# One decoder step on one core: the gate branch ahead of the fourth query tile, the recurrent channel sum ahead of the third key tile

## The reference, cut to what matters

```python
h = rms_norm(x, lp['norm1_g']) * (1.0 + scale1) + shift1
z = h @ lp['w_in']
x_lru, g_lru, q_lat, kv_lat, k_rope = jnp.split(z, IN_SPLITS, axis=-1)
hs, h_last = rg_lru(causal_dwconv(x_lru, ...), ...)          # scan over the tokens
lru_out = hs * jax.nn.gelu(g_lru)                            # the gate branch
q = (rms_norm(q_lat, ...) @ lp['w_uq'])                      # 8 heads, then q norm and rope
kv_lat = rms_norm(kv_lat, ...)                               # keys and values: kv_lat @ w_ukv
attn = attend(q_nope, q_rope, kv_lat, k_rope)                # prompt, and paged cache for the 8 sequences
mixed = jnp.concatenate([rms_norm(lru_out, lp['lru_out_norm_g']), rms_norm(attn, ...)]) @ lp['w_o']
x = x + gate1 * mixed
x = x + gate2 * ((gelu(gt) * val) @ lp['w_down'])            # behind norm2 and w_up with a short conv
```

## Time and profile before

| | us |
|---|---|
| median of 3 runs | 946.93 (945.82 to 947.53) |
| profiled execution, its own time | 949.23 |
| its span, first to last instruction | 947.4 |
| TensorE busy | 919.8 (97%) |
| VectorE busy | 637.4 (67%) |
| ScalarE busy | 513.1 (54%) |
| GpSimd busy | 184.3 (19%) |

### The profile page before, as it was taken

The page is one execution under the profiler, slowest core; times in us unless marked ns, Lnnn a source line. Parts: engine busy times, 40 slices in busy tenths (PEclk is TensorE's granted clock), DMA queues, the critical chain, the costliest instruction groups (busy, mean ns, idle before and its releaser), DMA issues.

```text
span 947.4 us, 20112 instructions
## 1 busy us (share of the span) xinstructions
PE 919.8 (97%) x7805; PEld 858.7 (91%) x7805; DVE 637.4 (67%) x1241; ACT 513.1 (54%) x1147; POOL 184.3 (19%) x163
## 2 busy tenths in 40 slices
PE   5899999999999999999999989999999999999998
PEld 3588876799999999999899979999999999999997
DVE  2893378488888888888863667777777777722321
ACT  2414845689889889898863354444444443311111
POOL 0032323333333324333330301100000001000000
PEclk9999999999999999999998999999999999999999
DMA  9996732300212203202130423333333331653202
GB/s 338 332 281 222 223 134 102 146 2 23 91 59 77 90 24 112 90 24 90 46 91 23 113 60 90 89 89 90 92 96 98 97 97 50 161 153 80 63 1 91
DMA packets 107897, 100.12 MB, mean 106 GB/s; under 512 B 7125, under 2 KB 96597, under 8 KB 105770
## 3 DMA queue, kind: packets, MB, share of 16 engines
q1 hardware_dynamic: 104030, 77.91, 28.1%
q0 software_dynamic: 3456, 20.97, 6.2%
q10 hardware_dynamic: 340, 0.27, 0.1%
HBM read 96.41 MB, written 2.94 MB: 105 GB/s over the span
## 4 chain that ended last, share of the span: by engine, by line
PE 88%; DVE 6%; ACT 2%; DMA 2%; issue 1%; SPq 0%; POOL 0%; DVEq 0%; ACTq 0%; POOLq 0%
PE ps L890 51%; PE ps L1286 20%; PE ps L885 6%; PE ps L1247 2%; PE ps L1183 2%; PE ps L923 2%; DMA RW<-w_ada 2%; PE ps L1062 1%; PE ps L896 1%; PE ps L1282 1%; DVE RB L1996 1%; PE ps L1209 1%; DVE input_low L1929 1%; DVE up_weights_low L2371 0%; DVE small L1970 0%
## 5 line engine op out<-in xcount | busy, mean ns | idle before, releaser
L890 PE MATMUL ps<-normed_high,up_weights_high 128*128 128x260 f32 x704 | 142.5, 284 | 2.5 <-DVE normed_low L2392 2.4
L890 PE MATMUL ps<-normed_high,up_weights_low 128*128 128x260 f32 x704 | 142.5, 284 | 0.0
L890 PE MATMUL ps<-normed_low,up_weights_high 128*128 128x260 f32 x704 | 142.1, 284 | 0.0
L1791 ACT ACTIVATE up_weights_high<-RW 128x1024 fp32r<-128x1024 f32 x44 | 46.6, 1061 | 128.0 <-PE ps L890 128.0
L836 POOL TENSOR_TENSOR latents_low<-RB,latents_high 128x512 fp32r<-128x512 f32 x64 | 82.7, 1292 | 165.7 <-ACT latents_high L1667 165.6
L1286 PE MATMUL ps<-key_weights_high,latents_high 128*128 128x260 f32 x512 | 113.3, 302 | 0.1
L890 PEld LDWEIGHTS ps<-normed_high,up_weights_high 128*128 128x128 f32 x704 | 108.9, 189 | 3.1 <-issue 2.2
L890 PEld LDWEIGHTS ps<-normed_high,up_weights_low 128*128 128x128 f32 x704 | 109.1, 189 | 0.0
L890 PEld LDWEIGHTS ps<-normed_low,up_weights_high 128*128 128x128 f32 x704 | 108.7, 189 | 0.0
L1286 PE MATMUL ps<-key_weights_high,latents_low 128*128 128x260 f32 x512 | 103.1, 283 | 0.0
L1286 PE MATMUL ps<-key_weights_low,latents_high 128*128 128x260 f32 x512 | 103.1, 283 | 0.0
(11 more groups left out here) (350 smaller groups left out, 2069.5 us busy)
## 6 DMA issues: line engine op xcount, KB each, us to landing
RW<-w_ada SPq DMA_DIRECT2D x24, 1024.0 KB, 7.0
RW<-w_up SPq DMA_DIRECT2D x44, 512.0 KB, 5.1
RW<-w_down SPq DMA_DIRECT2D x8, 1408.0 KB, 7.3
RW<-w_in SPq DMA_DIRECT2D x11, 512.0 KB, 6.4
RB<-w_o SPq DMA_DIRECT2D x8, 512.0 KB, 4.2
RB<-x_prompt SPq DMA_DIRECT2D x2, 1024.0 KB, 12.2
o_y_p<-RB SPq DMA_DIRECT2D x4, 448.0 KB
cst<-consts SPq DMA_DIRECT2D x1, 844.5 KB, 12.0
```

What stands on the lines that cost most here:

```text
L890: last = mm(ps[j % 4][rows[0]:rows[1], h, 0:H], lhsT, src[:, h * H:(h + 1) * H], start=start, stop=stop)
L1791: A(wuH[:, KT * g:KT * g + KT, :], wup[:, c, KT * g:KT * g + KT, :], ACT.Copy).then_inc(s_whi, 1)
```

## The change

The order of work on four engines is written differently; no product, sum or copy is added. TensorE issues four groups fewer: `keep_busy(spare, 3)` and four times `keep_busy(spare, 1)` are gone.

- TensorE: `w_in(11)` and the last chunk of w_ada stand ahead of `queries(3)`. The channel sum `J_NLRU` stands ahead of `keys_and_values(2)`, in PSUM buffer 3 instead of 1.
- ScalarE: the GELU stands ahead of the squares of query tile 3; `lru_squares` stand around that tile's root; the root of the channel sum stands ahead of the third key tile.
- VectorE: the fourth query tile and `mod_columns(5)` stand behind the product with the gate; `split_queries(0)` and `lru_normed` stand ahead of the copies into `QBD`.
- GpSimd: `kwL` is made there; the second sequence's gather stands behind the three additions.

The diff, cut:

```diff
+               "q2", "w11", "q3", "kv0", "kv1"])
+PREP_ORDER = [("c5", 3), ("qst", 3), ("nlru", 3), ("kv2", 1), ("qa", 3), ("kv3", 2), ("spread", 0), ("l0", 3), ("l1", 0),
+              ("l2", 3), ("l3", 0), ("l4", 3), ("l5", 0), ("l6", 3)]
...
+            pool.wait_ge(s_kw, 2)
+            for e in range(2):
+                nc.gpsimd.tensor_tensor(kwL[:, e, :, 0:4 * NOPE], wkn[:, :].rearrange("p (g n) -> p g n", g=2),
+                                        kwH[:, e, :, 0:4 * NOPE].bitcast(F32), ALU.subtract).then_inc(s_kw, 1)
...
-            for n in range(2):
-                cached_keys(n, n)
-                cached_latents(n, n)
-
+            cached_keys(0, 0)
+            cached_latents(0, 0)
+            nc.gpsimd.memset(QBD[:, :, :, :], 0.0).then_inc(s_bdz, 1)
             for k in range(1, LT):
...
+            cached_keys(1, 1)
+            cached_latents(1, 1)
...
             queries(2)
-            queries(3)
             w_in(11)
             later_chunk(15)
+            queries(3)
...
+            claim(pe, J_NLRU)
+            pe.wait_ge(s_lrn, LT - 1)
+            both(J_NLRU, ones, lru_sq[:, 0, :], True, True).then_inc(psum_full[J_NLRU % 4], 1)
             keys_and_values(2)
...
-            keep_busy(spare, 3)
             pe.wait_ge(s_kr, 2)
-            for a in range(4):
+            for a in range(5):
                 stored_rows(a)
-                keep_busy(spare, 1)
...
-            prep_squares(J_Q[3], query_sq, HEADS * QK)
-            prep_rstd(4, 2 * HEADS)
...
+            prep_squares(J_Q[3], query_sq, HEADS * QK)
+            act.wait_ge(s_lrud, 2)
+            lru_squares(0)
+            prep_rstd(4, 2 * HEADS)
+            lru_squares(2)
             key_squares(0)
             key_squares(1)
-            act.wait_ge(s_lrud, 2)
-            lru_squares(0)
             prep_rstd(5, HEADS)
-            lru_squares(2)
             prep_rstd(6, HEADS)
+            rstd(J_NLRU, LW).then_inc(s_rs, 1)
             key_squares(2)
...
+            prep_sums(3, query_sq, HEADS)
+            prep_query_tile(2)
+            mod_rows(5)
+            dve.wait_ge(s_g, 1)
+            V.tensor_tensor(GG[:, :, :], TA[:, :, :], GG[:, :, :], MUL).then_inc(s_lrud, 1)
+            prep_sums(4, query_sq, HEADS)
+            prep_query_tile(3)
             dve.wait_ge(s_kr, 2)
             dve.wait_ge(s_qtok, 4)
             V.tensor_copy(headk[NOPE:QK, :], krT[NOPE:QK, 0:NP]).then_inc(s_krk, 1)
...
-            mod_rows(5)
             mod_columns(5)
-            dve.wait_ge(s_g, 1)
-            V.tensor_tensor(GG[:, :, :], TA[:, :, :], GG[:, :, :], MUL).then_inc(s_lrud, 1)
             full(dve, J_QST)
...
             key_sums(2)
+            dve.wait_ge(psum_free[J_QA % 4], free_value(J_QA))
+            split_queries(0)
+            dve.wait_ge(s_rs, 5)
+            lru_normed()
             full(dve, J_SPREAD)
```

More of the change, by code:

```diff
@@ L1641, in _ @@
                 stored_rows(a)
-            rstd(J_NLRU, LW).then_inc(s_rs, 1)
             stored_rows(4)
@@ L2114, in _ @@
                 V.tensor_copy(kwH[:, e, :, 0:4 * NOPE], wk2).then_inc(s_kw, 1)
-            dve.wait_ge(s_kw, 2)
-            for e in range(2):
-                V.tensor_tensor(kwL[:, e, :, 0:4 * NOPE], wk2, kwH[:, e, :, 0:4 * NOPE].bitcast(F32), SUB).then_inc(s_kw, 1)
             mod_columns(4)
-            for a in range(2, 4):
-                prep_sums(1 + a, query_sq, HEADS)
-                prep_query_tile(a)
+            prep_sums(3, query_sq, HEADS)
[5 more added lines that the diff above has]
+            prep_query_tile(3)
             dve.wait_ge(s_kr, 2)
@@ L2139, in prep_keys, with lru_normed, split_queries @@
                 dve.sem_inc(psum_free[j % 4], 1)
-            mod_rows(5)
+            def lru_normed():
+                for k in range(LT):
+                    V.scalar_tensor_tensor(hT[:, k, :], GG[:, k, :], pr("lru_out_norm_g", k), rs[:, :], MUL, MUL).then_inc(s_mix, 1)
+            def split_queries(u):
+                e = u % 2
+                q = QA[:, u, :].rearrange("p (g h) -> p g h", g=2)
+                V.tensor_copy(kwH[:, e, :, 4 * NOPE:KWW], q).then_inc(s_kwq, 1)
+                dve.wait_ge(s_kwq, 2 * u + 1)
+                V.tensor_tensor(kwL[:, e, :, 4 * NOPE:KWW], q, kwH[:, e, :, 4 * NOPE:KWW].bitcast(F32), SUB).then_inc(s_kwq, 1)
             mod_columns(5)
-            dve.wait_ge(s_g, 1)
-            V.tensor_tensor(GG[:, :, :], TA[:, :, :], GG[:, :, :], MUL).then_inc(s_lrud, 1)
             full(dve, J_QST)
@@ L2171, in _ @@
             prep_keys(3)
-            def lru_normed():
-                for k in range(LT):
-                    V.scalar_tensor_tensor(hT[:, k, :], GG[:, k, :], pr("lru_out_norm_g", k), rs[:, :], MUL, MUL).then_inc(s_mix, 1)
             def by_key(x):
@@ L2216, in finish @@
                 V.tensor_copy(OLR[:, u - 1, :], bank("pv")[:, 0:KV]).then_inc(is_free("pv"), 1)
-            def split_queries(u):
-                e = u % 2
-                q = QA[:, u, :].rearrange("p (g h) -> p g h", g=2)
-                V.tensor_copy(kwH[:, e, :, 4 * NOPE:KWW], q).then_inc(s_kwq, 1)
-                dve.wait_ge(s_kwq, 2 * u + 1)
-                V.tensor_tensor(kwL[:, e, :, 4 * NOPE:KWW], q, kwH[:, e, :, 4 * NOPE:KWW].bitcast(F32), SUB).then_inc(s_kwq, 1)
             def row_max(u, name, blocks):
@@ L2314, in unit @@
                             split_queries(u + 1)
-            split_queries(0)
             for e in range(2):
@@ L2320, in _ @@
             st.seq(V.memset(new_scores[:, :, :], NEG))
-            dve.wait_ge(s_rs, 5)
-            lru_normed()
             for u in range(NS):
```

5 lines of the change are left out of this document (removed).

## The result

The changed kernel took 956.84 us in the median of 4 runs (953.97 to 958.91), the kernel before beside it 947.23 (945.82 to 949.31, 4 runs): ratio 1.0092, 95% interval 1.0071 to 1.0113. It is slower, by more than the 951.5 forecast and just outside the range (947.2 to 956.0).

What follows compares the result with a forecast made beforehand. TensorE was taken to bound the kernel, so only the start of the decode units (first key product) could move the time. Order +1.5, clock +1.6 and +1.5 gave +4.6 us on the 946.93 median: 951.5, range 947.2 to 956.

Steps and rivals of the forecast that it cites:

- two falls of the clock: TensorE's clock at 0.50 near 165, over channel sum and key tiles, and again near 180, into transposes and first keys.
- the second wait: TensorE ahead of the second stored tile: a wait of 2 us or more, released by VectorE's copies into QBD.
- order at full clock: TensorE up to the first transpose: the new order delays it from 178.45 to 180.0, +1.5 us.
- lock on SBUF: GpSimd additions beside VectorE's rotation of query tile 3, 161.0 to 165.2: taken as 0, at most one addition, 1.4 us.
- clock: TensorE's clock falling after the waits: 1.6 us over channel sum and key tiles, 1.5 over transposes and first keys.
- The wait ahead of `J_QST`: TensorE from 160.7, after the second key tile: waits about 4.4 us, released by VectorE's mod_columns(5).
- `kwL` on GpSimd: Moved to GpSimd, idle until 157.18: costs nothing, and gains nothing by taking some 1.2 us off VectorE ahead of a wait.
- The gathers: First sequence's 2.5 us earlier, nothing waiting; second's issued about 165 to 169, cost between 0 and 4.1 us, taken as 0.
- Full clock: Rival: TensorE's clock does not fall, or falls only where it waits anyway; +1.5 us, 948.4, chance 0.14.
- The tail doesn't matter: Rival: the loss before J_QA is all had back by dropped fillers, so tail order is indifferent; 946.9 us, chance 0.06.
- Low clock throughout: Rival: the clock stays low from 165 to the first keys; +7 to +9 us, 954 to 956, chance 0.13.
- Faster: Rival: the GELU chain's 2.5 us reach the units' start, J_QA ending before 167; 944.4 us, chance 0.06.

Runs made afterwards that it cites:

- e7_no_adds_fillers: Changed kernel without GpSimd's three additions, with 8, 3 and 5 fillers in TensorE's waits; 949.84 us, ratio 1.0012 to the kernel before.
- e3: Changed kernel with fillers in its waits: 10 ahead of J_QST, 3 ahead of the channel sum, 5 ahead of the second stored tile; 952.36 us, ratio 1.0052.
- e4_no_adds: Changed kernel without GpSimd's three additions, so three of four tiles are left out of the channel sum; 953.77 us, ratio 1.0078.
- e6_c5_first: Changed kernel with mod_columns(5) on VectorE straight behind the product with the gate, ahead of the fourth query tile; 956.20 us, ratio 1.0079.
- e5_qbd_first: Changed kernel with VectorE's copies into QBD and the last two key tiles ahead of split_queries(0) and lru_normed; 954.89 us, ratio 1.0066.
- e2_head_only: Kernel before with only the earlier half of the change (gate branch ahead of fourth query tile, kwL on GpSimd), tail and fillers as before; 957.32 us, ratio 1.0086.
- job A: Measuring job that ran the kernel before beside the first four follow-up kernels; the kernel before had a median of 946.98 us there.
- b1_product_late: Kernel before with VectorE's product with the gate behind the J_QST copies and first two key tiles, its squares behind the key squares; 946.23 us, ratio 0.9986.

## Why the prediction was wrong

The mechanism, its places and its sign were right: waits ahead of `J_QST` and ahead of the second stored tile with the named releasers, two falls of the clock near the named times, `J_QA` late, the units unchanged. The time was too small, and so were some of the marks that it named: `J_QA` started at 173.96, not at 169 to 171, and the first key product at 190.74, not by 190; the second wait was 1.89, just under the 2 named. By terms, each against the profiled execution of before, in us:

| term of the sum | forecast | measured | from |
|---|---|---|---|
| order at full clock | +1.5 | +1.3 | first transposes of e7_no_adds_fillers |
| lock on SBUF | 0, bound 1.4 | +2.1 | e3 less the row above (3.4 - 1.3); e4_no_adds: 2.1; rows: 2.0 |
| clock | +3.1 | +3.8 | changed kernel less e3 (33.33 - 29.51) |
| sum | +4.6 | +7.2 | distance |

**The step that failed is the lock.** The text had it in hand: additions at 161.0 to 165.2 beside the rotation (measured 161.41 to 165.53), and a rule of the Trainium skill, "SBUF — State Buffer", section "Who interferes with whom", that one of the two then waits. I took 0, as no row of before showed it beyond a DMA issue of 1.98 against 1.12 us, and bounded it by one addition. This case's runs agree with the rule: e4_no_adds takes the additions away and the two instructions are short again. The bound was wrong because two instructions each met an addition, and each ended only 0.29 and 0.15 us after the addition that it met: they paid what was left of it, 0.92 and 1.08 us more than alone. In e6_c5_first the first of them starts later against its addition (163.33, 0.45 us into it, instead of 0.22) and takes 1.13 instead of 1.35, ending the same 0.29 behind it. The products lasted about as long as an addition only because both started soon after theirs. The low end was chosen where the written conflict lay squarely on the path that I had named as the bound. With the 2.1 put in, the sum would have been 6.7 and the time 953.6: inside the range, but still 3.2 below the measured median, so this step is the largest that the runs show, not the whole miss.

**The clock was sized nearly right**, and by the right reason: e3_fillers changes nothing but what TensorE does in the waits, and gets back 3.8 us in the stretch and 4.5 in the medians. The falls were longer than the one of before (6.8 us each against 3.4); against e3_fillers, `J_QST` to `J_QA` took 2.2 us longer (6.63 and 4.40) and the second stored tile to the fillers 1.9 (6.79 and 4.85), each less than half a fall's length: part of the first lay over waiting, and in place of the second e3_fillers had small waits of its own. What sets off the second isn't shown: it comes without the wait of 1.89 too (e5_qbd_first), and one fall is left in e7_no_adds_fillers, where all three waits are filled.

**The wait ahead of `J_QST`** was put at 4.4 and was 6.11; less the 2.0 of the lock that is 4.1, and e4_no_adds shows 4.03. **`kwL` on GpSimd** took 2.54 us there instead of 1.29 on VectorE, at 147.80, where no wait points to it: it cost nothing, as said. **The gathers**: the second one issued at 165.69 to 169.2, as forecast, and no wait points to it.

**The rivals.** "Full clock" fell with the two falls. "The tail doesn't matter" is refuted by e5_qbd_first: the wait for `QBD` costs 1.3 in the stretch. "Low clock throughout" is what e2_head_only nearly did in its execution (0.50 from about 167 to 184), +11.1. "Faster" fell at the point that it named: `J_QA` ended at 175.91, not before 167.

**What stays open.** The medians differ by 9.6 us, the profiled stretches by 7.2, and 0.6 more is the later start of the first key tile; some 1.8 us are not seen in the pair of profiles. The pair is not typical: the changed kernel's lies 2.9 us below its median, that of before 2.0 above (949.23 against 947.23). The forecast had the same trouble, since its sum was made against the profile of before and put on the median. That the two profiled times differ by 4.7 us, nearly the 4.6 forecast, is luck: 7.9 us in the stretch and ahead of it, less 3.1 for a fall of before elsewhere. More or longer falls in the other runs would fit the 1.8. An estimate from the mean clocks, which counts a fall over waiting as well: a clock of 0.994, the median of before in the 16 runs of job A, leaves 5.7 us lost to the clock, and 0.9855, the middle of the changed kernel's four, some 13.8, which is 8 apart; in the profiled pair (0.991 and 0.987) it is 4. No trace shows the other runs.

## What to carry to other kernels

Before moving a step earlier on one engine, list what is then queued behind it there and who waits for that: here 2.5 us won for a branch that nobody waited for put 4.3 us of work ahead of what TensorE needed, and moving the same instruction the other way (b1_product_late) was worth 1.8 us in the stretch, though its time can't be told from that of the kernel before. Count a wait on the bounding engine by its length and by the clock after it, and put fillers into the wait, not behind it; then read the clock again, since one kernel with filled waits still had a fall. Where products of VectorE with both inputs in SBUF meet GpSimd additions, charge for every such product what is left of the addition that it meets, up to one whole addition each, and not one for the lot.

## What the runs showed of the hardware

- Two VectorE products with both inputs in SBUF, 0.43 and 0.28 us alone, took 1.35 and 1.36 beside GpSimd additions of 1.28 each, and ended 0.29 and 0.15 after the end of one; the additions kept their length (4.12 for three with the gaps, 4.14 before). Two VectorE products with one input in PSUM kept their 0.42 and 0.68 beside the same additions. The third and fourth instruction of the same rotation, behind the last addition, took 0.28 and 0.42.
- In the other direction GpSimd pays: the issue of an indirect DMA took 1.98 and 1.75 us (kernel before, e4_no_adds) beside the product of 2.33 us, and 0.93 to 1.12 elsewhere. In b1_product_late, where the product has moved away from it, the issue of 1.98 took 0.94.
- The granted clock stayed at 0.50 for 10 us in which TensorE was busy throughout (e2_head_only, 170 to 180), where some work was narrow products (8 columns, 3.58 us instead of 1.95) and the rest key tiles of 512 columns.
- With work in the waits the clock stayed at 1.00 through the same order of instructions (e3_fillers), and with two short waits less (0.60 and 0.33 us) the fall that the kernel before had was gone (b1_product_late). Filled waits were not enough in e7_no_adds_fillers, where the clock was at 0.50 once, from about 180.9 to 184.3.
